# Feed-forward of a two-part float32 network on one core: GpSimd's first low part without its wait for VectorE's sum of weights

## The chip, the core and the metric

The kernel runs on one core of a Trainium2 chip. A core has five engines that run their own instruction lists in order and wait for each other by semaphores: TensorE (PE in the profile, with the weight load as PEld), VectorE (DVE), ScalarE (ACT), GpSimd (POOL) and SyncE (SP), which here issues the loads of the weights. SBUF is the working memory, PSUM takes TensorE's results in eight banks. The metric is the device time of one execution in microseconds, lower is better.

## The reference

A sequence of 512 tokens with 1024 features goes through two blocks. The first has two layers, each feed-forward, mixer, feed-forward; the second has two layers, each a mixer, a cross-attention to a memory and a feed-forward. So there are six feed-forward stages, and they are what the change touches:

```
def _swiglu(x, w_gate, w_up, w_down):
    return (jax.nn.silu(x @ w_gate) * (x @ w_up)) @ w_down

x = x + MACARON * _swiglu(_rmsnorm(x, ffn1_norm), ffn1_w_gate, ffn1_w_up, ffn1_w_down)
...
def swiglu(h, w_gate_up, w_down):
    g, u = jnp.split(h @ w_gate_up, 2, axis=-1)
    return (jax.nn.silu(g) * u) @ w_down
```

The hidden width is 2816, that is 22 tiles of 128. Everything is float32.

## The kernel before, in words

Weights come as units of 128 x 1024 float32 (512 KB) through four slots of SBUF (`raws`), loaded by SyncE. A unit is split into a high part (`whi`, rounded to the type that TensorE multiplies fast) and a low part (`wlo`, the unit minus its high part), and a product is three matmuls: high weights by high and by low data, low weights by high data. ScalarE makes high parts (line 1218), GpSimd most low parts (`lo`, line 3121).

In most of a feed-forward stage a pair of units is not multiplied by eight block products but by seven (a 2 x 2 block scheme with seven products of sums of blocks). Such a pair is an item: `tile` m is the gate and up unit of hidden tile m, `down` a pair of units of the down projection. `SEQS[f]` lists the items of stage f: tiles up to 8, four down items (first run, 8 hidden tiles), tiles 9 to 14, four down items (second run, 6 hidden tiles, so 3/4 of the columns), tiles 15 to 21: 26 items in stage 0, 28 in the other five. The first tiles of a stage (4 in stage 0, else 2) are done in the plain way, and so is the third run of down units.

TensorE does the products of an item in the order 1, 5, 4 of the item before, then 6, 2, 3, 7 for a tile and 2, 6, 3, 7 for a down item (`seven`, matmuls in lines 640, 641 and 644). Products share two banks of PSUM, and between two products in one bank ScalarE takes a snapshot of what is there (line 1364): TensorE waits with product 6 for snapshot 1, with product 2 for snapshot 5, with product 7 for snapshot 6.

The sums of weight blocks for item s+1 are made while item s is multiplied. On VectorE an item's step is: the addition that closes the item before (`c22`, line 2233, or 2238 in a down item), for tiles behind an odd tile three small operations that make the turned hidden parts (lines 2299, 2301, 2303), then the sums:

```
dve.tensor_tensor(both(M.banks47[:, :], cols), both(M.raws[:, at + SEQ:at + 3 * SEQ], cols),
                  m21[:, None, :].to_broadcast([P, 2, cols]), ALU.add).then_inc(*S.tick("s13", f, s))
...
dve.tensor_tensor(bank[5][:, 0:cols], bank[4][:, 0:cols], m11, ALU.add).then_inc(*S.tick("s2", f, s))
...
dve.tensor_tensor(bank[6][:, 0:cols], bank[5][:, 0:cols], m12, ALU.add).then_inc(*S.tick("s4", f, s))
```

The first (line 2207, event `s13`, "the sum of weights") reads two slots of SBUF and writes PSUM; lines 2212 and 2214 read PSUM and SBUF. Then come the low part of the first sum (line 2219), the scaling of the gate (2272), the low part of the second (2225), the hidden product (2286) and the first row (2255, or 2259).

ScalarE's step is: the high part of the next item's first unit (1218), turned hidden high parts (1328), snapshot 1, the high part of the first sum (1335), snapshot 5 (for down items ahead of 1335), the high part of the second sum (1342), the high part of a block (1349), silu (1308), snapshot 6, hidden high parts (1314, 1324).

GpSimd's step is: the low part of the next item's first unit (`lo(first)`, line 3121), turned hidden low parts (3149), the scaling of silu (3129), for down items two partial additions (3157), the low part of a block of the second unit (`lo(second)`, line 3118), hidden low parts (3134, 3144). The order is written out by hand in the program of each engine; no scheduler moves anything.

Of the kernel before, what the change touches and what calls it, by code (L numbers as in the profile page):

```python
# [152 lines left out]
def rows(f, s):  # L153

    item = SEQS[f][s]
    if item[0] == "tile":
        return U["up", f, item[1]], U["gate", f, item[1]]
    return U["down", f, item[1], 2 * item[2]], U["down", f, item[1], 2 * item[2] + 1]
# [11 lines left out]
def turned_late(f, s):  # L170

    m = (SEQS[f][s - 1] if s else ("tile", PLAIN[f] - 1))[1] if s >= 0 and (not s or SEQS[f][s - 1][0] == "tile") else 0
    return m if m % 2 and m < PAIRED and m + 1 not in (F_PARTS[0][1], F_PARTS[1][1]) else 0
# [199 lines left out]
def seq(t, k, n=SEQ):  # L373
    return t[:, k * n:(k + 1) * n]
# [7 lines left out]
def turned_tile(T, p):  # L382

    e = p % 4
    return seq(T[f"tur{e // 2}h"], e % 2, 2 * SEQ), seq(T[f"tur{e // 2}l"], e % 2, 2 * SEQ)


def hidden_tile(M, T, m):

    if m >= PAIRED:  # L390
        k = m - PAIRED
        name, k = ("odd", (k + 3) % 4) if k < 4 else ("tur0", k - 4)
        return seq(T[name + "h"], k), seq(T[name + "l"], k)
    if m % 2:
        return seq(T["oddh"], m // 2 % 4), seq(T["oddl"], m // 2 % 4)
    e = m // 2 % 5
    if e == 0:
        return of_half(T["own"], 0), of_half(T["own"], 1)
    return of_half(M.gxh, 1, 2 * e - 2), of_half(M.gxl, 1, 2 * e - 2)


def hidden_cols(m):

    return HALF if m < PAIRED and m % 2 == 0 else SEQ
# [7 lines left out]
def of_half(t, half, k=0):  # L412

    return t[:, k * SEQ + half * HALF:k * SEQ + (half + 1) * HALF]
# [2679 lines left out]
def pool_program(pool, S, M):  # L3094
# [13 lines left out]
    def lo(u):  # L3108
        r = u % SLOTS
        if u in BY_VECTOR:  # L3110
            return
        pool.wait_ge(*S.at("hi", u))
        if u in BEHIND:
            pool.wait_ge(*S.at(*BEHIND[u]))
        if u in SEVEN and SEVEN[u][0] == 2:
            _, f, s = SEVEN[u]
            T = M.f[f]
            pool.tensor_tensor(seq(T[f"sl{s % 2}"], 0), seq(M.raw[r], 1), seq(T[f"sh{s % 2}"], 0).bitcast(F32),  # L3118
                               ALU.subtract).then_inc(*S.tick("lo", u))
            return  # L3120
        pool.tensor_tensor(M.wlo[r][:, :], M.raw[r][:, :], M.whi[r][:, :].bitcast(F32), ALU.subtract).then_inc(  # L3121
            *S.tick("lo", u))

    def ffn(f):
        T = M.f[f]

        def scale(m):
            pool.wait_ge(*S.at("silu", f, m))
            pool.tensor_tensor(T["s"][:, :], T["s"][:, :], M.R[:, :], ALU.mult).then_inc(*S.tick("silu_scaled", f, m))  # L3129

        def hidden_lo(m):
            hi, lo = hidden_tile(M, T, m)
            pool.wait_ge(*S.at("hh", f, m))
            pool.tensor_tensor(lo, T["u"][:, m % 2 * SEQ:m % 2 * SEQ + hidden_cols(m)], hi.bitcast(F32),
                               ALU.subtract).then_inc(*S.tick("hidden", f, m))

        def turned_hidden_lo(m):
            p = m // 2
            hi, lo = turned_tile(T, p)
            if m == F_PARTS[0][1]:  # L3140
                return
            if m % 2 == 0 or m - 1 == F_PARTS[0][1]:
                pool.wait_ge(*S.at("turned_h_hi_first", f, p))
                pool.tensor_tensor(lo[:, 0:HALF], M.xsd[:, 0:HALF], hi[:, 0:HALF].bitcast(F32), ALU.subtract).then_inc(
                    *S.tick("turned_h_lo_first", f, p))
            if m % 2 == 0:
                return
            pool.wait_ge(*S.at("turned_h_hi", f, p))
            pool.tensor_tensor(lo[:, HALF:], M.xsd[:, HALF:], hi[:, HALF:].bitcast(F32), ALU.subtract).then_inc(
                *S.tick("turned_h_lo", f, p))  # L3150

        def part(s, n, m, out, term):

            pool.wait_ge(*S.at(f"snap{n}", f, s))
            if SEQS[f][s][1]:
                pool.wait_ge(*S.at("part_sum", f, 0, m))
            pool.tensor_tensor(out, out, term, ALU.add).then_inc(*S.tick("part_pool", f, SEQS[f][s][1], m))

        def plain(m):
            lo(U["gate", f, m])  # L3160
            lo(U["up", f, m])

        plain(0)
        plain(1)
        for m in range(PLAIN[f] - 1):
            scale(m)
            if m + 2 < PLAIN[f]:
                lo(U["gate", f, m + 2])
                hidden_lo(m)
                turned_hidden_lo(m)  # L3170
                lo(U["up", f, m + 2])
            else:
                for u in rows(f, 0):
                    lo(u)
                hidden_lo(m)
                turned_hidden_lo(m)
        for s, item in enumerate(SEQS[f]):
            before = SEQS[f][s - 1] if s else ("tile", PLAIN[f] - 1)
            second = None
            if s + 1 < len(SEQS[f]):  # L3180
                first, second = rows(f, s + 1)
                pool.wait_ge(*S.at("s13", f, s + 1))
                lo(first)
            else:
                lo(U["down", f, 2, 0])
                lo(U["down", f, 2, 1])
            if turned_late(f, s - 1):
                turned_hidden_lo(turned_late(f, s - 1))
            if before[0] == "tile":
                scale(before[1])  # L3190
            if item[0] == "down":
                m = 2 * item[2]
                part(s, 5, m + 1, of_half(M.x, 1, m + 1), M.acc[:, 0:HALF])
                part(s, 6, m, seq(M.x, m), M.sq[:, :])
            if second is not None:
                lo(second)
            if before[0] == "tile":
                hidden_lo(before[1])
                if before[1] < PAIRED and turned_late(f, s) != before[1]:
                    turned_hidden_lo(before[1])  # L3200
        lo(U["down", f, 2, 2])
        scale(KF - 1)
        lo(U["down", f, 2, 3])
        hidden_lo(KF - 1)
        for m in range(4, KD):
            lo(U["down", f, 2, m])

    for key, u in U.items():
        if key[0] == "gate" and key[2] == 0:
            ffn(key[1])  # L3210
        elif key[0] not in ("gate", "up", "down"):
            lo(u)
# [210 lines left out]
```

## Time and profile before

| | us |
|---|---|
| median of 3 runs | 3106.76 (3106.54 to 3106.76) |
| the profiled execution | 3106.85 |
| its span, first to last instruction | 3105.6 |
| TensorE busy | 3080.5 (99%) |
| VectorE busy | 2168.9 (70%) |
| GpSimd busy | 1650.7 (53%) |
| ScalarE busy | 1624.8 (52%) |

An engine's busy time counts what its instructions take from start to end; an instruction that has started but cannot get at its data counts as busy too. Rows of a timeline give the start from the beginning of the span, the duration, the engine and line, what is written and read, and in brackets how long the engine had been idle and whose signal ended that.

### The profile page before, as it was taken

How to read it: one execution, taken by the hardware profiler on the slowest of the kernel's cores; microseconds unless marked ns; L12 is line 12 of the kernel's file. 1: busy time of each engine (PE TensorE's matmuls, PEld its weight loads, DVE VectorE, ACT ScalarE, POOL GpSimd, SP SyncE). 2: the span in 40 equal slices, each digit the busy share in tenths (PEclk: the TensorE clock that was granted, in tenths of full speed). 3: DMA queues.
4: the chain of work that ended last, by engine and by line, in shares of the span. 5: the costliest groups of instructions: out<-in, count | busy, mean ns of one | idle time of the engine just before them, and what ended most of it. 6: DMA issues, size and time to landing. Idle time of an engine off the chain costs nothing. (4 is left out here: it accounts for less than half of the span.)

```text
span 3105.6 us, 52754 instructions
## 1 busy us (share of the span) xinstructions
PE 3080.5 (99%) x20424; PEld 2827.1 (91%) x20424; DVE 2168.9 (70%) x2975; ACT 1624.8 (52%) x2567; POOL 1650.7 (53%) x994
## 2 busy tenths in 40 slices
PE   9999999999999999999999999999999999999999
PEld 8999888999989998888999877889999788889998
DVE  8776467877668774577877578558775786478773
ACT  6555433555556554335555455556554575455553
POOL 5676433677657675434767433226676112257674
PEclk9999999999999999999999999999999999999999
DMA  4323322232322232322223232322232223323232
GB/s 141 113 103 123 120 76 75 102 110 109 123 86 105 109 117 102 113 82 82 109 107 112 93 95 82 118 93 106 99 122 105 95 93 121 114 89 109 109 110 82
DMA packets 93320, 322.61 MB, mean 104 GB/s; under 512 B 10512, under 2 KB 14992, under 8 KB 93072
## 3 DMA queue, kind: packets, MB, share of 16 engines
q1 hardware_dynamic: 87680, 312.07, 28.5%
q10 hardware_dynamic: 5392, 7.17, 0.7%
q8 instruction: 164, 2.69, 0.4%
q14 instruction: 84, 0.69, 0.1%
HBM read 316.05 MB, written 2.10 MB: 102 GB/s over the span
## 5 line engine op out<-in xcount | busy, mean ns | idle before, releaser
L3121 POOL TENSOR_TENSOR wlo<-raws,whi 128x1024 fp32r<-128x1024 f32 x369 | 891.8, 2420 | 1135.8 <-ACT whi L1218 884.4
L1218 ACT ACTIVATE whi<-raws 128x1024 fp32r<-128x1024 f32 x422 | 441.0, 1051 | 159.2 <-PE bank L505 57.2
L3129 POOL TENSOR_TENSOR f_s<-f_s,R 128x512 f32<-128x512 f32 x132 | 172.4, 1306 | 193.8 <-ACT f_s L1308 192.4
L640 PE MATMUL bank<-gxh,whi 128*128 128x256 f32 x1064 | 268.8, 283 | 1.2 <-ACT acc L1364 1.2
L641 PE MATMUL bank<-gxl,whi 128*128 128x256 f32 x1064 | 268.6, 283 | 0.0
L2219 DVE TENSOR_TENSOR wlo<-banks,whi 128x1024 fp32r<-128x1024 f32 (+1 forms) x166 | 196.9, 1186 | 68.9 <-ACT whi L1335 68.9
L640 PE MATMUL bank<-f_th,f_sh 128*128 128x256 f32 x944 | 236.9, 283 | 0.0
L641 PE MATMUL bank<-f_tl,whi 128*128 128x256 f32 x944 | 236.7, 283 | 0.0
L640 PE MATMUL bank<-f_th,whi 128*128 128x256 f32 x944 | 236.7, 283 | 0.0
L641 PE MATMUL bank<-f_tl,f_sh 128*128 128x256 f32 x944 | 236.7, 283 | 0.0
L501 PE MATMUL bank<-gxh,whi 128*128 128x512 f32 x584 | 229.9, 394 | 1.4 <-DVE gxl L2161 1.4
L1335 ACT ACTIVATE whi<-banks 128x1024 fp32r<-128x1024 f32 (+1 forms) x166 | 165.2, 995 | 122.6 <-DVE banks L2212 122.2
L1364 ACT ACTIVATE sq<-bank 128x256 f32<-128x256 f32 x332 | 125.8, 379 | 194.9 <-PE bank L644 193.3
L502 PE MATMUL bank<-gxl,whi 128*128 128x512 f32 x584 | 227.4, 389 | 0.0
L3118 POOL TENSOR_TENSOR f_sl<-raws,f_sh 128x512 fp32r<-128x512 f32 x166 | 217.0, 1307 | 13.1 <-ACT f_sh L1349 13.1
L2207 DVE TENSOR_TENSOR banks<-raws 128x1024 f32<-128x1024 f32 (+1 forms) x166 | 210.0, 1265 | 0.0
L640 PEld LDWEIGHTS bank<-gxh,whi 128*128 128x128 f32 x1064 | 204.2, 192 | 1.8 <-ACT acc L1364 1.6
L641 PEld LDWEIGHTS bank<-gxl,whi 128*128 128x128 f32 x1064 | 204.2, 192 | 0.2
L2225 DVE TENSOR_TENSOR f_sl<-banks,f_sh 128x1024 fp32r<-128x1024 f32 (+1 forms) x166 | 195.3, 1176 | 0.0
L2286 DVE TENSOR_TENSOR f_u<-bank,f_s 128x512 f32<-128x512 f32 x132 | 91.3, 691 | 145.4 <-DVE f_sl L2225 83.7
L640 PEld LDWEIGHTS bank<-f_th,f_sh 128*128 128x128 f32 x944 | 181.2, 192 | 0.5 <-issue 0.2
L641 PEld LDWEIGHTS bank<-f_tl,f_sh 128*128 128x128 f32 x944 | 181.2, 192 | 0.2
(597 smaller groups left out, 9192.7 us busy)
## 6 DMA issues: line engine op xcount, KB each, us to landing
raws<-stream SPq DMA_DIRECT2D x588, 512.0 KB, 3.3
xa_mem<-memT ACTq DMA_DIRECT2D x2, 1024.0 KB, 6.2
m_dk<-decay ACTq DMA_DIRECT2D x2, 514.0 KB, 4.5
x<-xT ACTq DMA_DIRECT2D x4, 256.0 KB, 5.3
x<-xT SPq DMA_DIRECT2D x4, 256.0 KB, 6.6
outT<-x SPq DMA_DIRECT2D x2, 512.0 KB, 3.0
m_ct<-cos ACTq DMA_DIRECT2D x2, 256.0 KB, 2.6
m_sn<-sin ACTq DMA_DIRECT2D x2, 256.0 KB, 2.9
```

Source lines behind the costliest of these rows:

```text
L501: pe.matmul(out, seq(hi, k, P), h, start=first and k == 0, stop=False)
L502: pe.matmul(out, seq(hi, k, P), l, start=False, stop=False)
L640: pe.matmul(out, seq(hi, k, P), moving[k][0], start=first and k == 0, stop=False, skip_group_check=n != 1)
L641: pe.matmul(out, seq(hi, k, P), moving[k][1], start=False, stop=False, skip_group_check=n != 1)
L1218: act.activation(M.whi[r][:, :], M.raw[r][:, :], ACT.Copy).then_inc(*S.tick("hi", u))
L1335: act.activation(both(M.whi[u % SLOTS][:, :], cols), both(M.banks47[:, :], cols), ACT.Copy).then_inc(*S.tick("s13_hi", f, s))
L2207: dve.tensor_tensor(both(M.banks47[:, :], cols), both(M.raws[:, at + SEQ:at + 3 * SEQ], cols), m21[:, None, :].to_broadcast([P, 2, cols]), ...
L2219: dve.tensor_tensor(both(M.wlo[r][:, :], cols), both(M.banks47[:, :], cols), both(M.whi[r][:, :].bitcast(F32), cols), ALU.subtract).then_i ...
L2225: dve.tensor_tensor(both(T[f"sl{s % 2}"][:, SEQ:], cols), both(M.banks56[:, :], cols), both(T[f"sh{s % 2}"][:, SEQ:].bitcast(F32), cols), ...
L3118: pool.tensor_tensor(seq(T[f"sl{s % 2}"], 0), seq(M.raw[r], 1), seq(T[f"sh{s % 2}"], 0).bitcast(F32), ALU.subtract).then_inc(*S.tick("lo", u))
L3121: pool.tensor_tensor(M.wlo[r][:, :], M.raw[r][:, :], M.whi[r][:, :].bitcast(F32), ALU.subtract).then_inc(*S.tick("lo", u))
L3129: pool.tensor_tensor(T["s"][:, :], T["s"][:, :], M.R[:, :], ALU.mult).then_inc(*S.tick("silu_scaled", f, m))
```

## The change

GpSimd waited for the sum of weights of item s+1 (`s13`) before it made the low part of that item's first unit. The wait is taken out. What remains in front of the low part is the wait for the high part of the same unit (in `lo`). The low part and the sum don't touch each other's results: the sum reads the slots, the low part reads a slot and the high part. The slot is given back to SyncE as before, only when both the low part and VectorE's sums have been made. No instruction is added, removed or moved on any engine.

```
@@ -3179,7 +3179,6 @@
             second = None
             if s + 1 < len(SEQS[f]):
                 first, second = rows(f, s + 1)
-                pool.wait_ge(*S.at("s13", f, s + 1))
                 lo(first)
             else:
                 lo(U["down", f, 2, 0])
```

## Rows read from the trace of the kernel before

**Rows 1.** The page, sections 1 and 2: busy time, and granted clock.
```profile
PE 3080.5 (99%) x20424; PEld 2827.1 (91%) x20424; DVE 2168.9 (70%) x2975; ACT 1624.8 (52%) x2567; POOL 1650.7 (53%) x994
...
PEclk9999999999999999999999999999999999999999
```

**Rows 2.** Waits: who waited, for whom, us in total, times, longest.
```profile
POOL wlo L3121 <- DVE banks L2207: 244.0, 130, 5.3
```

**Rows 3.** VectorE's groups by form: busy us, mean ns of one, idle before.
```profile
L2207 DVE TENSOR_TENSOR banks<-raws 128x1024 f32<-128x1024 f32 x142 | 184.4, 1299 | 0.0
...
L2212 DVE TENSOR_TENSOR banks<-banks,raws 128x512 f32<-128x512 f32 x142 | 99.3, 699 | 4.9
```

**Rows 4.** Timeline from 44 us on, VectorE and then GpSimd: start, duration, instruction.
```profile
44.31 1.51 DVE L2303 SCALAR_TENSOR_TENSOR xsd<-xsd,f_u 128x256 f32<-128x256 f32 x1
...
47.53 2.19 DVE L2207 TENSOR_TENSOR banks<-raws 128x1024 f32<-128x1024 f32 x1
...
44.23 1.30 POOL L3134 TENSOR_TENSOR f_oddl<-f_u,f_oddh 128x512 fp32r<-128x512 f32 x1 [0.47 <-ACT f_oddh L1314]
46.77 1.86 POOL L3149 TENSOR_TENSOR f_tur0l<-xsd,f_tur0h 128x768 fp32r<-128x768 f32 x1 [1.24 <-ACT f_tur0h L1328]
48.60 3.38 POOL L3121 TENSOR_TENSOR wlo<-raws,whi 128x1024 fp32r<-128x1024 f32 x1
```

**Rows 5.** Timeline of tile 18 in stage 2, engine by engine.
```profile
1153.67 1.23 DVE L2207 TENSOR_TENSOR banks<-raws 128x1024 f32<-128x1024 f32 x1
1154.93 0.70 DVE L2212 TENSOR_TENSOR banks<-banks,raws 128x512 f32<-128x512 f32 x1
...
1152.00 1.31 POOL L3134 TENSOR_TENSOR f_oddl<-f_u,f_oddh 128x512 fp32r<-128x512 f32 x1 [0.27 <-ACT f_oddh L1314]
1154.98 2.41 POOL L3121 TENSOR_TENSOR wlo<-raws,whi 128x1024 fp32r<-128x1024 f32 x1 [1.67 <-DVE banks L2207]
...
1156.59 0.38 ACT L1364 ACTIVATE acc<-bank 128x256 f32<-128x256 f32 x1
...
1158.89 0.28 PE L640 MATMUL bank<-gxh,whi 128*128 128x256 f32 x1
```

**Rows 6.** Timeline of tile 7 in stage 2, behind the odd tile 5.
```profile
970.98 0.74 DVE L2299 SCALAR_TENSOR_TENSOR xsd<-f_u,xsd 128x256 f32<-128x256 f32 x1
971.64 0.41 DVE L2301 TENSOR_TENSOR xsd<-f_u 128x256 f32<-128x256 f32 x1
...
972.32 1.22 DVE L2207 TENSOR_TENSOR banks<-raws 128x1024 f32<-128x1024 f32 x1
...
970.15 1.30 POOL L3134 TENSOR_TENSOR f_oddl<-f_u,f_oddh 128x512 fp32r<-128x512 f32 x1 [0.27 <-ACT f_oddh L1314]
...
969.98 1.04 ACT L1218 ACTIVATE whi<-raws 128x1024 fp32r<-128x1024 f32 x1
...
975.23 0.38 ACT L1364 ACTIVATE acc<-bank 128x256 f32<-128x256 f32 x1
...
976.20 0.28 PE L640 MATMUL bank<-gxh,whi 128*128 128x256 f32 x1
```

**Rows 7.** Timeline of tile 11 in stage 2.
```profile
1051.62 0.41 DVE L2299 SCALAR_TENSOR_TENSOR xsd<-f_u,xsd 128x256 f32<-128x256 f32 x1
...
1052.62 1.23 DVE L2207 TENSOR_TENSOR banks<-raws 128x1024 f32<-128x1024 f32 x1
...
1055.54 0.38 ACT L1364 ACTIVATE acc<-bank 128x256 f32<-128x256 f32 x1
...
1056.84 0.28 PE L640 MATMUL bank<-gxh,whi 128*128 128x256 f32 x1
```

**Rows 8.** Timeline of tile 13 in stage 2.
```profile
1076.34 0.38 ACT L1364 ACTIVATE acc<-bank 128x256 f32<-128x256 f32 x1
...
1077.00 0.28 PE L640 MATMUL bank<-gxh,whi 128*128 128x256 f32 x1
```

**Rows 9.** TensorE's groups: busy us, mean ns, idle before and its releaser.
```profile
L640 PE MATMUL bank<-f_tur0h,f_sh 128*128 128x256 f32 x192 | 50.7, 286 | 6.2 <-DVE x L2238 6.1
```

More of the change, by code:

```diff
@@ L3181, in ffn @@
                 first, second = rows(f, s + 1)
-                pool.wait_ge(*S.at("s13", f, s + 1))
                 lo(first)
```

## Prediction

> **What bounds the kernel now.** I read the page first, then the waits, the groups by form, and then timelines of single items in the feed-forward stages. The page shows TensorE busy for 3080.5 of 3105.6 us at a granted clock of nine tenths or more in every slice [rows 1]: it is the bound, and any time that another engine saves is worth nothing unless TensorE waits for it. The reader is to see next that the wait in question is large for GpSimd: 130 times, 244.0 us in all, it stood before a low part until VectorE's sum of weights had ended [rows 2], that is 1.88 us each. The one place in every feed-forward stage where TensorE really waits in front of a product is the second item of the second run of down units, 6.2 us over the six stages, released by VectorE's last addition of the item before [rows 9]; everything else in the items runs back to back.
>
> So the question is not what GpSimd gains, but what the earlier low part does to VectorE. The sum of weights (line 2207) takes 1.22 us in the undisturbed case; its mean is 1299 ns; a low part takes 2.41 us [rows 3, 5].
>
> **The two engines exclude each other.** In the timeline from 43 us on GpSimd starts a subtraction at 44.23 that ends at 45.53; VectorE's line 2303, which reads two tensors in SBUF, starts at 44.31 and ends at 45.82, in 1.51 us [rows 4], where its sister line 2301 with the same shape and two SBUF inputs takes 0.41 us [rows 6]. It did nothing until GpSimd was done, and then needed 0.29 us. The sum of weights also reads two SBUF tensors: at 47.53 it starts under GpSimd's line 3149, which ends at 48.63, and it ends at 49.72, 1.09 us later; GpSimd's next low part, issued at 48.60, takes 3.38 us instead of 2.41 and ends at 51.98, 2.26 us after the sum [rows 4]. Two rules follow: whoever holds the path when the other comes keeps it to its end, and between waiting instructions the one that came first is next. VectorE's operations that read PSUM and one SBUF tensor are not held up: line 2212 has a mean of 699 ns over 142 of them, the same as in the undisturbed item [rows 3, 5].
>
> The Trainium skill ("Advanced Engine Details and Errata", VectorE Performance Modes, Mode Summary) says that GpSimd and VectorE block each other for VectorE instructions in the modes that use both read ports; float32 tensor_tensor with a PSUM output isn't one of them, so by that sentence alone the sum of weights could not be blocked and the change would cost nothing. The 1.51 and 2.19 us above contradict it. The skill's "SBUF — State Buffer" (Who interferes with whom) counts two SBUF inputs in as well, and what it states gives the sum below.
>
> **What the change does, part by part.** It removes one wait from 160 low parts (25 in the first stage, 27 in each of the other five); nothing is added or moved. The low part then starts when its high part (ScalarE, line 1218) and GpSimd's instruction before it have ended. Three kinds of item:
>
> (a) Items where GpSimd is busy past the sum, or comes free while the sum already waits (even tiles of the first run, most down items of the second run): the sum is first in the queue as now, cost 0, gain at most 0.15 us of GpSimd time each.
>
> (b) Plain items: tiles from 17 on, and down items of the first run. GpSimd's previous instruction ends at 1153.31, the sum starts at 1153.67 [rows 5]. The low part would start at about 1153.35, hold the path until 1155.76, and the sum would end 1.09 us later, at 1156.85 instead of 1154.90: 1.95 us late. Behind it on VectorE stand lines 2212 and 2214, on ScalarE the high part of the sum (line 1335) and then the snapshot of product 5, which TensorE needs before product 2. That snapshot ends at 1156.97 and product 2 starts at 1158.89: 1.92 us of cover [rows 5]. Late by 1.95, with 0.05 to 0.08 us from a signal to the next engine's start (1154.90 to 1154.98 for GpSimd): about 0.1 us. After such an item GpSimd's own tail is late and the sum wins the next ones, so I count 0.3 us per stage for the five such tiles, 0.25 for tile 9, and 0 for the down items, where the snapshot stands ahead of the high part on ScalarE.
>
> (c) Items behind an odd tile whose turned hidden parts are made late: there VectorE does three small two-input operations (lines 2299, 2301, 2303) ahead of the sum. GpSimd's hidden low part ends at 971.45, the first of the three, which waited for it, at 971.72, and the high part has been there since 971.02 [rows 6]. The low part is queued at 971.49 and gets the path at 971.72, ahead of line 2301; by the 2.26 us of rows 4 it ends at 973.98, line 2301 ends 0.29 us later, at 974.27 instead of 972.05: all that follows is 2.2 us late. Snapshot 5 ends at 975.61 and product 2 starts at 976.20, so the cover is 0.59 us [rows 6]. TensorE loses 2.2 - 0.59 + 0.06, some 1.7 us, part of it already at product 6, since the snapshot of product 1 stands behind the turned high part on ScalarE and moves too. The remaining 0.5 us of lateness stays as I take it: the even tile between runs through the same chain from sum to hidden low part, on which nothing waits for TensorE, so the next odd tile has no cover left and loses the full 2.2.
>
> The sum per stage. Odd tiles of the first run: stages 1 to 5 have three, 1.7 + 2.2 + 2.2 = 6.1; stage 0 has two behind its longer plain part, which I count like the later ones, 4.4; together 34.9 us. Tile 11: line 2299 starts at 1051.62; GpSimd is free some 0.36 us before VectorE's turn, as in rows 5 (1153.31 against 1153.67), and its low part has the path. So the sum, now ending at 1053.85, is 2.2 us late; cover from 1055.92 to 1056.84, 0.92 us; loss 1.3, and 0.1 at tile 12 [rows 7]. Six times 1.4 is 8.4. Tile 13: late by 2.2 plus some 0.75 left from tile 11, cover 1076.72 to 1077.00, 0.28 us [rows 8]; loss 2.7, six times 16.2. The small ones: 0.3 + 0.25 and 0.25 at the entry of the down items (their additions are late by what is left over), 0.8 per stage, 4.8. In all 34.9 + 8.4 + 16.2 + 4.8 = 64 us, 60 of them from 29 items.
>
> The profiled execution took 3106.85 us (span 3105.6), the median of the runs is 3106.76; so 3106.8 + 64 = **3171 us**, slower by 2.1%.
>
> Bounds. If the lateness of an item were absorbed before the next one, every odd tile would pay only 1.7, and tiles 11 and 13 only 1.3 and 2.0: 17 x 1.7 + 6 x 3.3 + 2, some 51 us. If only the first odd tile of a stage paid, because TensorE's own delay then sets the others apart, it would be 6 x (1.7 + 3.3), 30 us. That the low part gets in only behind the three small operations changes little: the sum, starting at 972.32 now, would end at 972.32 + 2.26 + 1.09 = 975.67 instead of 973.54, 2.1 us late. Above, a further 0.3 to 1 us in each of the eight down items of a stage, where TensorE already waits for such an addition [rows 9], would add 15 to 30 us. I take 64 because both queue rules are read from this kernel's own instructions.
>
> **Rivals.**
> 1. *The lateness is smaller, or is absorbed* (3137 to 3158, the 30 to 51 us above). For it: ScalarE and VectorE are not the busiest engines. Against it: a cover of 0.59 us in the odd tile of rows 6 beside 1.92 in the plain item of rows 5 says how little is regained there even now.
> 2. *No effect* (3107): VectorE is served before GpSimd's queued instruction, or the product covers hold. For: the case at 47.53, where VectorE won. Against: it had come first there; at 44.23 GpSimd came first by 0.08 us and kept the path for 1.30.
> 3. *Faster*, the other side: GpSimd's low part, 1.9 us earlier, pulls its whole queue forward (scaling, second low part, partial sums), and the wait at rows 9, whose chain goes through GpSimd, goes: at most 6.2 us, 3101. It decides if the three items ahead of it let GpSimd gain over 1 us; but there GpSimd is behind its high parts and not behind the sum, and a sum that is late takes the gain back.
> 4. *Much slower* (3200 to 3350): every one of the 130 items pays its 1.9 us, up to 244 us, because the weights' next loads or the down items fall behind too. Against: cover of 1.92 us in the plain ones, and sums are needed a whole item later.
>
> **How the numbers follow.** The forecast has 0.72, rival 1 0.12, rival 2 0.05, rival 3 0.03, rival 4 0.08. The forecast's own range is 3158 to 3185. The range 3135 to 3197 takes in rival 1 and leaves out rivals 2 and 3 and rival 4, 0.16 in all. About 0.2% (6 us) is what a measurement of this kernel tells from no change: slower by more 0.93, within 0.04, faster 0.03.
>
> **What would show it.** Right: GpSimd's wait for line 2207 is gone from the waits; the mean of line 2207 rises from 1.30 towards 2.5 us in plain items and line 2301's from 0.41 towards 1.1 or more; TensorE has idle time before products 6 and 2 (lines 640), released by ScalarE's snapshots (line 1364), of 1 to 2.5 us in 29 items and hardly any in tiles 17 to 21; the granted clock stays. Wrong: line 2207 keeps 1.22 us, or its delays appear and TensorE's gaps don't.

## Result and profile after

| | before | after |
|---|---|---|
| median of the runs (us) | 3106.76 | 3174.63 (3174.46 to 3174.92) |
| ratio to before, 95% interval | | 1.0219 [1.0205, 1.0233] |
| span of the profiled execution (us) | 3105.6 | 3173.6 |

The change costs 67.9 us; 64 were forecast. The page of the changed kernel, sections 1 and 2, answers to [rows 1]:

```profile
PE 3104.0 (98%) x20424; PEld 2836.4 (89%) x20424; DVE 2302.9 (73%) x2975; ACT 1623.5 (51%) x2567; POOL 1707.7 (54%) x994
...
PEclk9999999999999999999999999999999999999999
```

The instructions are the same in number. The digits of the clock are those of before, but a slice is 79 us long and hides two short falls: the granted clock is 0.5 (1.2 GHz) from 72.1 to 75.5 us and from 628.5 to 631.9 us, where the kernel before has its full 2.4 GHz (falls of 6.8 us near 1770 and 1810 us and at the very end are in both). What they cost is taken up behind the experiments. Two stretches of the changed kernel, one in the first fall and one at the same place of stage 2 (busy us of PE, PEld, DVE, ACT and POOL, clock, share of DMA, GB/s):

```profile
72.20:75.50 3.30, 3.30 (x16) 3.04 (x16) 2.94 (x4) 3.03 (x6) 0.62 (x2) 0.50 0.00 0
980.00:983.00 3.00, 2.70 (x23) 2.50 (x22) 2.64 (x4) 2.81 (x6) 0.32 (x2) 1.00 0.02 5
```

VectorE is busy for 134 us more: that is not work, but operations that stand still while they are counted as busy. Its groups by form (busy us, mean ns, idle before) answer to [rows 3]:

```profile
L2207 DVE TENSOR_TENSOR banks<-raws 128x1024 f32<-128x1024 f32 x142 | 248.3, 1749 | 0.1
L2212 DVE TENSOR_TENSOR banks<-banks,raws 128x512 f32<-128x512 f32 x142 | 99.3, 699 | 4.9
...
L2301 DVE TENSOR_TENSOR xsd<-f_u 128x256 f32<-128x256 f32 x42 | 66.9, 1592 | 0.0
L2299 DVE SCALAR_TENSOR_TENSOR xsd<-f_u,xsd 128x256 f32<-128x256 f32 x42 | 53.2, 1266 | 0.4
```

The mean of the sum of weights has gone from 1299 to 1749 ns, that of line 2301 from 413 to 1592 ns. Line 2212, with one operand in PSUM, kept its 699 ns to the nanosecond.

GpSimd's wait of [rows 2] is gone from the waits, and TensorE has waits for ScalarE's snapshots in front of line 640, of which the kernel before has 1.2 us in all. The third row, VectorE's line 2238, is the stall of [rows 9]. First GpSimd's longest and then TensorE's (who, for whom, us in total, times, longest):

```profile
POOL wlo L3121 <- ACT whi L1218: 895.3, 199, 105.2
```

```profile
PE bank L640 <- ACT sq L1364: 37.5, 30, 1.9
PE bank L640 <- ACT acc L1364: 9.1, 28, 0.9
PE bank L640 <- DVE x L2238: 6.3, 6, 1.1
```

The first two rows make 46.6 us, less than was lost. TensorE's busy time rose as well, by 23.5 us for the same 20424 matmuls: the last matmul before a gap is drawn 0.16 us into it (0.28 us long, where the next would start after 0.12), and the second behind a gap starts up to 0.1 us late. So I measured losses by item: within a product matmuls start 0.12 us apart, and what lies between product starts beyond that is lost. By this count the kernel before loses 10.7 us in its items and the changed one 77.5 us: 66.8 us more, nearly all of the 68.0 us by which the span grew.

One item in full: tile 7 of stage 2, the place of [rows 6]. VectorE, GpSimd, ScalarE and TensorE in the timeline (start, duration, instruction, idle before):

```profile
995.40 0.43 DVE L2233 TENSOR_TENSOR bank<-bank,acc 128x256 f32<-128x256 f32 x1 [0.19 <-PE bank L644]
995.74 1.18 DVE L2299 SCALAR_TENSOR_TENSOR xsd<-f_u,xsd 128x256 f32<-128x256 f32 x1
996.85 2.62 DVE L2301 TENSOR_TENSOR xsd<-f_u 128x256 f32<-128x256 f32 x1
999.38 0.41 DVE L2303 SCALAR_TENSOR_TENSOR xsd<-xsd,f_u 128x256 f32<-128x256 f32 x1
...
995.34 1.30 POOL L3134 TENSOR_TENSOR f_oddl<-f_u,f_oddh 128x512 fp32r<-128x512 f32 x1 [0.27 <-ACT f_oddh L1314]
996.59 2.59 POOL L3121 TENSOR_TENSOR wlo<-raws,whi 128x1024 fp32r<-128x1024 f32 x1
...
999.83 0.84 ACT L1328 ACTIVATE f_tur1h<-xsd 128x768 fp32r<-128x768 f32 x1 [3.62 <-DVE xsd L2303]
1000.58 0.37 ACT L1364 ACTIVATE sq<-bank 128x256 f32<-128x256 f32 x1
...
1001.09 0.35 PE L640 MATMUL bank<-f_th,f_sh 128*128 128x256 f32 x1 [1.42 <-ACT sq L1364]
...
1003.06 0.39 PE L640 MATMUL bank<-gxh,whi 128*128 128x256 f32 x1 [0.30 <-ACT acc L1364]
```

Line 2299 stands still until GpSimd's line 3134 is done at 996.64, and ends 0.28 us later. The low part was queued at 996.59, before line 2301, and has the path until 999.18; line 2301 ends 0.29 us behind it. ScalarE's turned high part, the snapshot of product 1 behind it, and TensorE's product 6 follow. Each waits for the one before. Most of an item's loss is in front of product 6, behind snapshot 1 (1.6 us here), and 0.53 us in front of product 2.

### The profile page after: what moved, and what is told of

Read it like the earlier page. It is cut to its first block and busy times, and to the rows that moved or that the text cites. A ratio compares the mean times of both kernels' runs of the same rounds, so it can differ in the third digit from the quotient of the medians.

```text
span 3173.6 us, 52594 instructions
## 1 busy us (share of the span) xinstructions
PE 3104.0 (98%) x20424; PEld 2836.4 (89%) x20424; DVE 2302.9 (73%) x2975; ACT 1623.5 (51%) x2567; POOL 1707.7 (54%) x994
## 5 line engine op out<-in xcount | busy, mean ns | idle before, releaser
L3121 POOL TENSOR_TENSOR wlo<-raws,whi 128x1024 fp32r<-128x1024 f32 x369 | 948.2, 2573 | 902.8 <-ACT whi L1218 895.3
L2207 DVE TENSOR_TENSOR banks<-raws 128x1024 f32<-128x1024 f32 (+1 forms) x166 | 276.0, 1662 | 0.1
```

## Experiments

The theory: GpSimd's subtractions and VectorE's operations with two SBUF operands never run at the same time; whoever comes first keeps the path to its end, and the next is whoever has waited longest. As an engine has at most one operation waiting in these rows, none of them tells this from taking turns. The loss arises where a low part now gets in ahead of VectorE's late pair: the three turned sums (lines 2299, 2301, 2303) that VectorE makes in front of the sum of weights in 29 of the items.

**Where the loss sits.** `late_only` takes the wait away in those 29 items alone, `others_only` everywhere else:

```
-                pool.wait_ge(*S.at("s13", f, s + 1))
+                if not turned_late(f, s - 1):      # others_only: without the "not"
+                    pool.wait_ge(*S.at("s13", f, s + 1))
```

> The wait is gone only in the items that hold VectorE's two late turned sums of a pair of hidden tiles in front of the weight sum (five per stage, 29 in the program; in the other 100 or so it stays). Theory (SBUF is read two operands at a time by one engine alone, and GpSimd's low part now gets in between VectorE's operations): the losses sit in these items, 1.76 + 2.23 + 2.21 + 1.87 + 2.20 us a stage, so about +60 us, 3163 to 3171 us. Rival (GpSimd's low part over the sum costs something in every item): 29 of 130 items, so about +15 us, 3122 us.

> The wait is gone everywhere but in those 29 items. Theory: the sum is late in each of these items (3.2 us in place of 1.2) but TensorE is not, save 0.24 + 0.29 + 0.2 us a stage, so +3 to +7 us, 3110 to 3114 us. Rival of the spread loss: about +53 us, 3160 us.

Measured: 3167.6 us, 1.0194 [1.018, 1.0208], and 3111.89 us, 1.0015 [1.0006, 1.0025]: 60.8 and 5.1 us, together 65.9 of the 67.9. The loss is in the 29 items, and the rival of a loss spread over all items is refuted. Of the 2 us that the two runs leave, 1.4 are in tile 11: it loses 1.63 us in `late_only` and 1.87 in the changed kernel, six times. Another 0.4 are the two falls of the clock, which neither run has. `others_only` shows both halves of the theory in its groups (VectorE's lines 2207 and 2301), since the first is held up as much as in the changed kernel and the second not at all:

```profile
L2207 DVE TENSOR_TENSOR banks<-raws 128x1024 f32<-128x1024 f32 x142 | 248.5, 1750 | 0.0
...
L2301 DVE TENSOR_TENSOR xsd<-f_u 128x256 f32<-128x256 f32 x42 | 17.3, 413 | 0.0
```

So 64 us (248.5 - 184.4) of VectorE's standing still in the sum cost 5 us of the kernel. In the changed kernel another 49.5 us in line 2301 (66.9 - 17.4) and 20 in line 2299 (53.2 - 33.1) cost 60.

**The order, not the overlap.** `in_front` lets the low part run beside the sum, but not ahead of it:

```
-                pool.wait_ge(*S.at("s13", f, s + 1))
+                if turned_late(f, s - 1):
+                    pool.wait_ge(*S.at("turned_h", f, turned_late(f, s - 1) // 2))
+                elif s:
+                    pool.wait_ge(*S.at("c22", f, s - 1))
```

> GpSimd's low part waits for VectorE's instruction in front of the weight sum (the last turned sum of a late pair, else the closing of the item before) instead of the sum itself. The low part may thus start over the sum, but not over the turned sums. Theory (order at the shared path): nothing of the late pair is pushed back; at worst the sum itself stands behind the low part, 2 us late in every item, of which a late item passes on about what tile 9's does, so 3105 to 3125 us. Rival (that the two run at once is what costs, whatever stands first): as without any wait, about 3165 us.

Measured: 3104.75 us, 0.9993 [0.9984, 1.0003], the same as before. Its timeline in tile 7 of stage 2, VectorE and GpSimd:

```profile
971.38 0.41 DVE L2303 SCALAR_TENSOR_TENSOR xsd<-xsd,f_u 128x256 f32<-128x256 f32 x1
971.71 1.22 DVE L2207 TENSOR_TENSOR banks<-raws 128x1024 f32<-128x1024 f32 x1
...
971.87 3.33 POOL L3121 TENSOR_TENSOR wlo<-raws,whi 128x1024 fp32r<-128x1024 f32 x1 [1.03 <-DVE xsd L2303]
```

The sum comes 0.16 us ahead of the low part and is not touched; the low part is the one that is stretched, from 2.41 to 3.33 us, and ends 2.27 us after the sum, as if it had waited. Line 2303 ends at 971.79: VectorE's next instruction starts 0.08 us before that, GpSimd, which needs a signal, 0.08 us after, and that decides who is first.

**What the path is.** The next kernels give VectorE's operations one operand in PSUM. They leave out the true second operand and so compute other values; sizes and order are the same:

```
+            second = M.banks47[:, :] if s > 1 else M.raws[:, at + SEQ:at + 3 * SEQ]
-            dve.tensor_tensor(both(M.banks47[:, :], cols), both(M.raws[...], cols), m21..., ALU.add)
+            dve.tensor_tensor(both(M.banks47[:, :], cols), both(second, cols), m21..., ALU.mult if s > 1 else ALU.add)
...                                  # the all_psum pair only:
+            third = [bank[5][:, 0:HALF]] * 3 if m > PLAIN[f] else [parts[0], h12, h21]
-            dve.scalar_tensor_tensor(parts[2], h22, -1.0, parts[0], ...)
+            dve.scalar_tensor_tensor(parts[2], h22, -1.0, third[0], ...)   # parts[1], parts[3] alike
```

> Leaves out part of the computation: from the third item of a stage on, VectorE's weight sum reads its second operand from PSUM in place of the weights, and the three late turned sums read theirs from PSUM too; sizes and order are the same. GpSimd's wait stays. Both theories: the sum as long as before or some tenths shorter (1.2 us for the usual item), total 3095 to 3112 us. It is the base for the next kernel.

> The same with GpSimd's wait gone. Theory (the price is that VectorE's operations with two SBUF operands can't run beside GpSimd's): with one operand in PSUM there is nothing left to wait for, so within 5 us of the kernel with the wait, and the sum's mean stays at about 1.2 us. Rival (the low part comes too early, or GpSimd's traffic as such slows VectorE and the rest): +50 us or more over the kernel with the wait, as between the two kernels of this case.

> As the last, but only the weight sum reads its second operand from PSUM; the late turned sums read two SBUF operands as in the kernel before. GpSimd's wait is gone. Theory: the sum is no longer held up, the turned sums are: about 0.4 to 1.4 us of each late item's 1.8 to 2.2 us stay, so +15 to +45 us over the kernel with the wait and PSUM operands. Rival (only the sum's own delay counts): no loss.

Measured: 3101.06 us, 0.998 [0.9971, 0.9989]; 3112.83 us, 1.0018 [1.0008, 1.0027]; and 3157.43 us, 1.0162 [1.0146, 1.0177]. Against the kernel with the wait it is 11.8 us more with all operands changed, in place of 67.9, and 56.4 us with the sum's alone (that one has no base of its own; 3101.06 us stands for it). Both miss their expectation, the first by 7 us, the second by 11. The first miss has a reason in the edit: the first late pair of a stage kept its two SBUF operands, and it alone lost time (1.76 us in each of stages 1 to 5 and 2.2 in stage 0, 11.0 of the 11.8). The timeline of `all_psum_free` has both kinds side by side. The changed pair, tile 7 of stage 2:

```profile
974.38 0.41 DVE L2301 SCALAR_TENSOR_TENSOR xsd<-f_u,banks 128x256 f32<-128x256 f32 x1
974.71 0.41 DVE L2303 TENSOR_TENSOR xsd<-f_u,banks 128x256 f32<-128x256 f32 x1
975.04 0.41 DVE L2305 SCALAR_TENSOR_TENSOR xsd<-xsd,banks 128x256 f32<-128x256 f32 x1
975.37 1.23 DVE L2208 TENSOR_TENSOR banks<-banks,raws 128x1024 f32<-128x1024 f32 x1
...
974.15 2.41 POOL L3123 TENSOR_TENSOR wlo<-raws,whi 128x1024 fp32r<-128x1024 f32 x1
```

and the unchanged one, tile 3:

```profile
932.98 2.61 DVE L2303 TENSOR_TENSOR xsd<-f_u 128x256 f32<-128x256 f32 x1
...
932.74 2.58 POOL L3123 TENSOR_TENSOR wlo<-raws,whi 128x1024 fp32r<-128x1024 f32 x1
```

Four operations of VectorE at their full speed beside a low part that takes its usual 2.41 us, against one that needs 2.61. That is the theory: not SBUF traffic as such, but VectorE's second SBUF operand. `sum_psum_free` loses 1.62 to 1.91 us in each late item past the first of a stage (once 2.25), where I had left 0.4 to 1.4: a sum that can't be held up shortens the loss by no more than 0.3 us, because the loss is made in front of it. The changed kernel's own trace says so already: in tile 7 of stage 2 its sum of weights starts at 999.72 and takes its full-speed 1.22 us. The Trainium skill ("SBUF — State Buffer", Who interferes with whom) states just this, that a VectorE instruction with two SBUF inputs contends with a GpSimd instruction that reads SBUF, and that one with at most one SBUF input, outside the two-port modes, doesn't; the trace agrees on both halves, 2.61 against 0.41 us. The Trainium skill's list of modes that the prediction weighed ("Advanced Engine Details and Errata", VectorE Performance Modes, Mode Summary) doesn't name the case, but doesn't exclude it either, so the prediction's word "contradict" is too strong; the rows decide.

**The size.** Both start from the changed kernel, in the 29 items: `half_size` makes 512 of the low part's 1024 columns and leaves the others out, `two_halves` makes all of them in two operations.

```
+        if half:                     # half = turned_late(f, s - 1)
+            pool.tensor_tensor(M.wlo[r][:, 0:SEQ], M.raw[r][:, 0:SEQ], ...)   # two_halves: and [:, SEQ:2 * SEQ]
```

> The changed kernel, and in the 29 items with a late pair GpSimd's low part makes 512 of its 1024 columns (the other half of the low part is left out). Theory (VectorE's next operation stands still for as long as the low part runs): the low part takes 1.3 in place of 2.4 to 2.6 us, so the items of tiles 3, 5, 7, 11 and 13 lose about 0.7, 1.1, 1.1, 0.8 and 1.1 us in place of 1.76 to 2.23; over the program 30 to 35 us are given back, about 3141 us. Rival (a fixed price for changing hands): no change, 3174 us.

> The changed kernel, and in the same items the low part is made in two operations of 512 columns, one behind the other. Theory of a queue in which VectorE's waiting operation comes between the two: the first half holds up one turned sum, the second the next, the total is the same, 3168 to 3180 us. Rival (the second half comes too late to get in between the turned sums, or the first leaves enough slack): as with half the columns, about 3141 us. Rival two (VectorE gets no turn between the halves): as the changed kernel, with the second turned sum alone held up.

Measured: 3141.75 us, 1.0113 [1.0099, 1.0127], and 3174.01 us, 1.0216 [1.02, 1.0231]. Tiles 3, 5, 7, 11 and 13 of stage 2 lose 0.62, 1.09, 1.09, 0.76 and 1.09 us at half the size. In two pieces they lose what they lost in one. VectorE of `two_halves` in tile 7 of stage 2:

```profile
996.68 1.51 DVE L2301 TENSOR_TENSOR xsd<-f_u 128x256 f32<-128x256 f32 x1
998.11 1.51 DVE L2303 SCALAR_TENSOR_TENSOR xsd<-xsd,f_u 128x256 f32<-128x256 f32 x1
```

Each half holds up one operation by 1.1 us (0.41 at its full speed): the engines take turns, and a shorter operation does not help when another stands behind it.

**The mis-sized term.** In tile 11's item GpSimd has a second operation ready, the first half of a turned low part (line 3144). `hold_turned` is the changed kernel with one more wait in front of it:

```
             if m % 2 == 0 or m - 1 == F_PARTS[0][1]:
+                if m % 2:
+                    pool.wait_ge(*S.at("turned_h", f, p))
```

> The changed kernel, and GpSimd's first half of a turned low part in tile 11's item (one per stage, the operation behind the low part) waits for the last sum of the late pair. Theory (this second GpSimd operation of 0.93 us slips in too, before VectorE's second turned sum): the item loses about 1.4 in place of 1.87 us, so some 2 to 3 us in all, 3172 us. Rival (it has no part in the loss): 1.87 us stays.

Measured: 3171.29 us, 3.3 us less than the changed kernel; tile 11's item loses 1.31 us in place of 1.87, which six times is 3.3 us.

**A stall of the kernel before.** `close_first` reorders VectorE at the place of [rows 9], `both_orders` adds `in_front` to it:

```
             if s:
                 c22(s - 1)
+            if s and SEQS[f][s - 1] == ("down", 1, 0):
+                first_row(s - 1)
...
-            first_row(s)
+            if SEQS[f][s] != ("down", 1, 0):
+                first_row(s)
```

> The wait stays as before. Once a stage, at the first two down items, VectorE closes the second half row of the first item before it closes the first row of the second (which waits for a product that comes late), so that the copy which TensorE waits for is released sooner. TensorE loses 1.24 us at this place in each of six stages before: about -6 to -7 us, 3100 us, if the order of the two is its cause; if the cause is TensorE's own bank or the product's end, no change, 3107 us.

> Two correct edits of the kernel before together: GpSimd's low part waits for VectorE's instruction in front of the weight sum, and at the first two down items VectorE closes the first item's second half row before the second item's first row. Alone they stand at 0.9993 and 0.9999 of before; the first takes 0.25 us a stage from the loss at the second down item, the second moves 0.5 us of it to the third item. Together 3101 to 3105 us, if the two add; 3104 to 3107 if the loss only moves on.

Measured: 3106.55 us, 0.9999 [0.999, 1.0008], and 3104.72 us, 0.9996 [0.9988, 1.0005]. The forecast of 6 us fails: the second down item loses 0.73 in place of 1.24 us, and the third now 0.47. The stall moves on. The count by item gives `in_front` 1.6 us less than the kernel before and `both_orders` 1.7, so the second edit adds nothing to the first. No version here that computes the same is measurably faster than the kernel before.

## Why the prediction was right, and where it was off

- *TensorE bounds, and its clock stays.* Right but for the two falls of 3.4 us, which the prediction did not have and which cost 0.4 us in all (below). What GpSimd gained (244 us of waiting) was worth nothing.
- *The two queue rules.* Right. That the first to come is served first, and between waiting ones the longest waiting, is borne out by `in_front`, `two_halves` and tile 7 above; that one holds the path to its end by tile 7 too; that PSUM operands are exempt by `all_psum_free`.
- *Plain items (b).* The sum's delay is right and so is its harmlessness. Expected 0.3 us a stage for tiles from 17 on and 0.25 for tile 9; measured 0.29 and 0.24. The entry of the down items and the items around it, expected 0.25 a stage or 1.5 us, made 1.7 us in all. The third down item of stage 3 lost another 1.5 us, once, by the same queue: there the low part came 0.19 us ahead of the sum, in stage 2 it came 0.16 us behind it. VectorE and GpSimd of the changed kernel, stage 3 and then stage 2:

```profile
1698.60 3.03 DVE L2207 TENSOR_TENSOR banks<-raws 128x768 f32<-128x768 f32 x1
1698.41 2.39 POOL L3121 TENSOR_TENSOR wlo<-raws,whi 128x1024 fp32r<-128x1024 f32 x1
...
1141.57 1.04 DVE L2207 TENSOR_TENSOR banks<-raws 128x768 f32<-128x768 f32 x1
1141.73 3.14 POOL L3121 TENSOR_TENSOR wlo<-raws,whi 128x1024 fp32r<-128x1024 f32 x1
```

  The delayed sum sets back ScalarE's step, and product 7, which waits for snapshot 6, starts 1.4 us late. The prediction had counted most down items of the second run at nothing, as items in which the sum comes first. Small terms: 6.4 us for 4.8.
- *Odd tiles of the first run.* Stages 2 to 5: expected 1.7 + 2.2 + 2.2, measured 1.76 + 2.23 + 2.21. Stages 0 and 1 lost 0.2 and 0.5 us more than that count, of which the clock has 0.2 in each. In all 36.1 us for 34.9. The prediction priced an item by the cover in front of product 2; most of the loss appears at product 6 already, as it had allowed, and the sum is the same.
- *Tile 11.* The step that failed: 1.3 us expected, 1.87 measured; with the 0.1 expected for tile 12, which lost nothing, 11.2 us for 8.4. The prediction let one GpSimd operation in. The timeline of the changed kernel in stage 2 shows two:

```profile
1079.02 2.50 DVE L2299 SCALAR_TENSOR_TENSOR xsd<-f_u,xsd 128x256 f32<-128x256 f32 x1
1081.44 0.95 DVE L2301 TENSOR_TENSOR xsd<-f_u 128x256 f32<-128x256 f32 x1
...
1078.84 2.40 POOL L3121 TENSOR_TENSOR wlo<-raws,whi 128x1024 fp32r<-128x1024 f32 x1
1081.19 0.93 POOL L3144 TENSOR_TENSOR f_tur0l<-xsd,f_tur0h 128x256 fp32r<-128x256 f32 x1
```

  The low part holds up line 2299, line 3144 then comes before line 2301 and holds it up by another 0.54 us. Holding it back gave 1.31 us, the prediction's figure.
- *Tile 13.* 2.7 expected, 2.2 measured, 13.2 us for 16.2. I had let 0.75 us of tile 11's lateness arrive at tile 13; with a cover of 0.28 us the measured loss leaves some 0.3 for it. In tiles 5, 7 and 13 the loss is the same 2.2 us, the lateness of one low part.

The terms add to 66.8 us; the misses of tiles 11 and 13 are of one size, 3 us up and 3 down, so that by luck the total was nearer than its parts.

Tile 5 of stages 0 and 1 stands out: 3.84 and 3.50 us, with only 1.24 and 1.45 in tile 7, where other stages have 2.23 and 2.21. In `hold_turned`, whose edit does not touch these tiles, they lose 2.70 and 2.19 us in stage 0 (0.49 of the 2.70 are lost in the kernel before too) and 2.54 and 2.23 in stage 1, and nearly the same in `late_only`. The trace shows what differs: TensorE's clock, and not the queue. In stage 0 VectorE's, ScalarE's and GpSimd's rows of the item are alike in both, 0.06 us apart, but in the changed kernel the granted clock fell to 0.5 at 72.1 us, and the matmuls of product 2 start 0.21 us apart in place of 0.12. The changed kernel and then `hold_turned`:

```profile
73.57 0.41 PE L640 MATMUL bank<-gxh,whi 128*128 128x256 f32 x1
73.79 0.41 PE L641 MATMUL bank<-gxl,whi 128*128 128x256 f32 x1
...
73.50 0.28 PE L640 MATMUL bank<-gxh,whi 128*128 128x256 f32 x1
73.62 0.28 PE L641 MATMUL bank<-gxl,whi 128*128 128x256 f32 x1
```

Tile 7 pays less behind it, as TensorE is then further behind the other engines, and the net price is 0.2 us in each of the two stages. `two_halves` has the same two falls. Before the falls TensorE had stood idle for 1.93 and 1.79 us, in the tiles without one for at most 1.45; but in `hold_turned` it stood idle for 1.92 and 1.76 us at the same places and kept its clock. What tips it is open, and so is why stage 1 loses 0.3 us more in tile 5 than the later stages even at the full clock.

## What to carry to other kernels

A wait that seems to cost its engine 244 us can be what keeps a shared path free for the engine that counts. Before removing one, list what will then run beside the freed instruction, and for each whether both need the path: two engines' operations that exclude each other are to be planned as one queue, and the order in it set by a signal of the instruction in front, with the urgent ones first. Splitting the less urgent operation changed nothing, as its pieces followed each other; making it smaller did: half the columns took about 1.1 us off nearly every one of the 29 losses, 33 of the 68 us in all.

## What was unexpected

- A blocked instruction shows as busy, not as waiting: the page puts VectorE's share up from 70% to 73% and lists no wait. Only a mean that rises with the shape unchanged (413 to 1592 ns) tells it. TensorE's matmuls at half the clock look alike: busy, and longer at the same shape (0.41 for 0.28 us), while the page's clock line shows nines throughout.
- A delay of the same size costs 5 us in one place and 60 in another. The first has 1.92 us of cover before TensorE's next product [rows 5] and the second 0.59 and less [rows 6].
- With PSUM in place of its second SBUF operand the sum's mean fell from 1299 to 1222 ns. The sum itself is no shorter, an undisturbed one takes 1.22 to 1.23 us in the kernel before too [rows 5, 6]; it is the sums held up by GpSimd that are gone from the mean. The kernel with the wait became 5.9 us faster (0.998 [0.9971, 0.9989]); the stall at the second down item fell from 1.24 to 0.28 us. That operand carries weights, so this is a pointer, not a version.
